# Gated recurrence, sparse and local attention in one transformer block: the recurrence's scores in column strips of 32 tokens, with its decays multiplied in place

## What is computed

```
f = lb + (1 - lb) * sigmoid(fp);  k = (1 - lb) * sigmoid(-fp)
b = cumsum(log f)
decay = exp(where(causal, b_i - b_j, -1e30))         # per channel d
scores_ij = sum_d q_id * decay_ijd * k_jd
o_i = sum_j scores_ij * v_j + (q_i * exp(b_i)) @ state
```

```
score = sum over 8 index heads of iw_h * relu(iq_h . ik)      # 64 channels per index head
keep the 64 largest scores of each row, softmax over those, times the compressed values
```

## Time and profile before

| | |
|---|---|
| median of 3 runs | 493.51 us |
| the profiled execution's own time | 493.7 us |
| its span | 491.9 us |
| TensorE busy (matmul) | 476.9 us, 97% of the span |
| TensorE weight loads | 398.2 us, 81% |
| VectorE busy | 306.7 us, 62% |
| ScalarE busy | 236.5 us, 48% |
| GpSimd busy | 64.8 us, 13% |
| mean granted TensorE clock | 0.991 |

### The profile page before, as it was taken

One profiled execution on the slowest core, in us unless ns is written; L12 is line 12 of the kernel. 1 busy time (PEld: TensorE's weight loads), 2 busy tenths in 40 slices (PEclk: granted clock), 3 DMA queues, 4 the chain that ended last, 5 costly groups with the idle time before them and its releaser, 6 DMA issues.

```text
span 491.9 us, 5942 instructions
## 1 busy us (share of the span) xinstructions
PE 476.9 (97%) x2292; PEld 398.2 (81%) x2292; DVE 306.7 (62%) x405; ACT 236.5 (48%) x330; POOL 64.8 (13%) x54
## 2 busy tenths in 40 slices
PE   7999999996999999999999999999999999999995
PEld 6888778885888888888888886888888888888884
DVE  5657679978447765467537787584644645643432
ACT  4948367162436555544455155565354453533520
POOL 0421001995470020000000000000000000000000
PEclk9999999997999999999999999999999999999999
DMA  8987635341233535566865634755565656565302
GB/s 299 401 254 215 190 128 172 113 139 50 85 111 107 182 117 171 172 193 216 282 205 178 204 102 164 228 199 176 182 200 173 197 185 183 190 228 179 122 0 85
DMA packets 25728, 85.71 MB, mean 174 GB/s; under 512 B 3011, under 2 KB 4580, under 8 KB 25700
## 3 DMA queue, kind: packets, MB, share of 16 engines
q1 hardware_dynamic: 24888, 84.39, 52.9%
q10 hardware_dynamic: 812, 0.95, 0.5%
HBM read 84.08 MB, written 1.25 MB: 173 GB/s over the span
## 4 chain that ended last, share of the span: by engine, by line
PE 84%; DVE 10%; ACT 2%; issue 1%; DMA 1%; DVEq 0%; ACTq 0%
PE bank L1262 75%; PE bank L1286 4%; DVE wl L700 3%; PE bank L1435 1%; DVE work L834 1%; DVE top L832 1%; PE bank L1376 1%; DMA cols<-cols_in 1%; ACT wh L428 1%; DVE prob L892 1%; PE bank L1407 1%; DVE prob L878 1%; PE bank L1349 1%; PE bank L1358 1%; ACT prob L532 1%
## 5 line engine op out<-in xcount | busy, mean ns | idle before, releaser
L700 DVE TENSOR_TENSOR wl<-raw,wh 128x1024 fp32r<-128x1024 f32 (+2 forms) x152 | 184.6, 1247 | 79.3 <-ACT wh L428 78.7
L428 ACT ACTIVATE wh<-raw 128x1024 fp32r<-128x1024 f32 (+2 forms) x152 | 153.7, 1046 | 62.1 <-PE bank L1262 62.0
L1262 PE MATMUL bank<-wh,hTh 128*128 128x512 f32 (+1 forms) x432 | 171.7, 398 | 2.0 <-DVE hTl L720 0.9
L1262 PE MATMUL bank<-wl,hTh 128*128 128x512 f32 (+1 forms) x432 | 167.8, 388 | 0.0
L1262 PE MATMUL bank<-wh,hTl 128*128 128x512 f32 (+1 forms) x432 | 167.7, 388 | 0.0
L1262 PEld LDWEIGHTS bank<-wh,hTh 128*128 128x128 f32 x432 | 81.6, 189 | 20.0 <-issue 1.3
L1262 PEld LDWEIGHTS bank<-wh,hTl 128*128 128x128 f32 x432 | 81.5, 189 | 16.8
L1262 PEld LDWEIGHTS bank<-wl,hTh 128*128 128x128 f32 x432 | 81.7, 189 | 15.2
L1198 POOL TENSOR_TENSOR st<-st 128x1 f32<-128x1 f32 x4 | 2.2, 549 | 290.9 <-DVE st L1107 170.9
L1262 PE MATMUL bank<-wh,fTh 128*128 128x512 f32 x88 | 34.7, 395 | 0.0
L1262 PE MATMUL bank<-wh,fTl 128*128 128x512 f32 x88 | 34.5, 392 | 0.0
(11 more groups left out here) (186 smaller groups left out, 486.3 us busy)
## 6 DMA issues: line engine op xcount, KB each, us to landing
raw<-w_stream SPq DMA_DIRECT2D x148, 512.0 KB, 3.6
raw<-w_stream SPq DMA_DIRECT2D x4, 328.0 KB, 8.6
x<-x_in SPq DMA_DIRECT2D x4, 256.0 KB, 5.6
bias<-bias_scratch SPq DMA_DIRECT2D x8, 128.0 KB, 5.1
x<-x_in SPq DMA_DIRECT2D x1, 1024.0 KB, 5.8
out<-mo SPq DMA_DIRECT2D x4, 256.0 KB, 2.0
post<-post_mix ACTq DMA_DIRECT2D x1, 512.0 KB, 8.7
fg<-pre_ffn SPq DMA_DIRECT2D x1, 512.0 KB, 6.6
```

The costliest lines, as they stand in the source:

```text
L428: did(act.activation(wh[:, u % SPLIT, a:2 * w], raw[:, u % RING, a:2 * w], ACT.Copy), high_done, u + 1)
L700: did(dve.tensor_tensor(wl[:, u % RING, a:2 * w], raw[:, u % RING, a:2 * w], wh[:, u % SPLIT, a:2 * w].bitcast(F32), ALU.subtract), low_do ...
L1262: ins = pe.matmul(bank[bk][:, 0:w], lhs[:, kt, t * P:(t + 1) * P], rhs[:, k], start=first, stop=final)
```

## The change

Five things change, all in front of the first gate block; the units, their order and all that follows are the same.

1. **Strips.** `diag` and the levels 1 to 16 are computed in strips of 32 tokens: for each head and token tile, four matmuls with 32 stationary columns (the strip's k) and 32 or 16 moving ones (the strip's q), which write partitions 32j to 32j + 31 of PSUM. Level 32 takes 16 matmuls of 32 by 32, level 64 takes 8 of 64 by 64, level 128 is as before. The scores of the levels up to 16 go into a compact tile `near` (128 x 8 x 32), which ScalarE spreads into `tri` at the end (`spread_near`); `tri` is cleared by GpSimd early on.
2. **In place.** GpSimd keeps `kT` and `qp` (q times gates) and multiplies the lower halves of one and the upper halves of the other by one gate product per half; the products of the halves (`f_up`) are one small multiplication per level. So a level can be built only when TensorE has finished the one before.
3. **Two units apart.** The levels now stand two units apart on TensorE, and the "d" attention's probabilities, values, and the "m" attention's logits move behind levels 32, 64 and 128; `mP` moves behind `ho`.
4. **Scaling and normalising on ScalarE.** The gates' scaling (8 operations) and the division by the sums (8 operations for each attention) move from VectorE to ScalarE; VectorE keeps the reciprocal (`invert_sums`).
5. **Indexer by row halves.** The matmuls of an even and an odd index head alternate, into two banks.

```diff
@@ tensor: indexer
-            for i in range(6):
-                if i % 2 == 0:
-                    units(15 + i // 2)
-                ps = begin(f"ix{i}")
-                t, its_heads = INDEXER[i]
-                w = 512 // len(its_heads)
-                for k, h in enumerate(its_heads):
+            for i in range(0, 6, 2):
+                units(15 + i // 2)
+                pair = [begin(f"ix{i}"), begin(f"ix{i + 1}")]
+                t, n = INDEXER[i][0], len(INDEXER[i][1])
+                w = 512 // n
+                for k in range(n):
+                    for ps, (_, its_heads) in zip(pair, INDEXER[i:i + 2]):
+                        h = its_heads[k]
...
@@ tensor: diag and level
+            tokens_of = [(h * TT + t, h, t) for h in range(H) for t in range(TT)]
+            ps = begin("diag")
+            for c, h, t in tokens_of:
+                for j in range(0, P, STRIP):
+                    at = slice(t * P + j, t * P + j + STRIP)
+                    ins = pe.matmul(ps[j:j + STRIP, c * STRIP:(c + 1) * STRIP], kT[:, h, at], hqT[:, h, at], start=True, stop=True)
...
-                for t in range(TT):
-                    for h in range(H):
-                        a_h = att[i % 2][:, h, t * P:(t + 1) * P]
-                        upper = a_h.rearrange("p (g two k) -> p g two k", two=2, k=w)[:, :, 1, :]
-                        at = t * S + h * P // 2
-                        ins = pe.matmul(ps[:, at:at + P // 2], a_h, upper, start=True, stop=True)
+                for c, h, t in tokens_of:
+                    if w in IN_STRIP:
+                        for j in range(0, P, STRIP):
+                            at = slice(t * P + j, t * P + j + STRIP)
+                            upper = qp[:, h, at].rearrange("p (g two k) -> p g two k", two=2, k=w)[:, :, 1, :]
+                            ins = pe.matmul(ps[j:j + STRIP, c * HALF_STRIP:(c + 1) * HALF_STRIP], kT[:, h, at], upper, start=True, stop=True)
+                    else:
+                        for j in range(0, P, 2 * w):
+                            a = t * P + j
+                            ins = pe.matmul(ps[j:j + w, c * w:(c + 1) * w], kT[:, h, a:a + w], qp[:, h, a + w:a + 2 * w], start=True, stop=True)
@@ gpsimd
-            for i, w in enumerate(LEVELS + [P]):
...
-                did(pool.tensor_tensor(a_lo, k_lo, s_lo, ALU.mult))
-                did(pool.tensor_tensor(a_up, q_up, p_up, ALU.mult), s["level_built"], i + 1)
...
-                    did(pool.tensor_tensor(s_lo, s_lo, p_up[:, :, w - 1:w].to_broadcast([P, g, w]), ALU.mult))
...
-                    did(pool.tensor_tensor(p_up, p_up, p_lo[:, :, w - 1:w].to_broadcast([P, g, w]), ALU.mult))
+            did(pool.memset(tri[:], 0.0), tri_zeroed, 1)
...
+            did(pool.tensor_tensor(qp[:], hqT[:], pre[:], ALU.mult), s["level_built"], 1)
+            for i, w in enumerate(LEVELS):
...
+                f_lo, f_up = (f[:, :, w - 1:w] for f in halves(pre[:], w))
+                wait_job(pool, f"L{w}")
...
+                did(pool.tensor_tensor(k_lo, k_lo, f_up.to_broadcast([P, g, w]), ALU.mult))
+                did(pool.tensor_tensor(q_up, q_up, f_lo.to_broadcast([P, g, w]), ALU.mult), s["level_built"], i + 2)
...
+                    did(pool.tensor_tensor(f_up, f_up, f_lo, ALU.mult))
@@ scalar
+            for h in range(H):
+                did(act.activation(kT[:, h], kT[:, h], ACT.Copy, scale=stat(OML + h)))
+                did(act.activation(pre[:, h], pre[:, h], ACT.Identity, bias=stat(LB + h), scale=stat(OML + h)), gates_scaled, h + 1)
...
+            def normalise(k):
+
+                act.wait_ge(sums_inverted, k + 1)
...
+                        ins = act.activation(row, row, ACT.Copy, scale=stat(RCP + 8 * k + t * H + h))
...
+                    did(act.activation(tri4[sl, :, 0:3:2, sl], near[sl].rearrange("p (h t) k -> p h t k", t=TT), ACT.Copy), tri_near, n + 1)
@@ vector: level
+                if w in IN_STRIP:
...
+                    did(dve.copy_predicated(upper, mask, src), *job_read(f"L{w}"))
+                    return
...
+                    ins = dve.tensor_copy(tri4[j:j + w, :, 0:3:2, j + w:j + 2 * w], src)
```

More of the change, by code:

```diff
@@ L200, in build_block @@
         pre = sb("pre", [P, H, S], stack=early)
-        suf = sb("suf", [P, H, S], stack=early)
-        att = [sb(f"att{i}", [P, H, S], stack=early) for i in range(2)]
+        qp = sb("qp", [P, H, S], stack=early)
+        near = sb("near", [P, H * TT, STRIP], stack=early)
         tri = sb("tri", [P, H, TW], stack=early)
@@ L939, in _ @@
             low_until(44)
-            normalise(1)
+            logits("m", 1, 0)
+            maxima(1)
             low_until(45)
@@ L1459, in _ @@
                 transposes(f"mqT{i}", tiles(stage[:, 2], 2 * i))
-            units(33)
+            units(34)
             level(4)
-            units(34)
-            level(5)
             units(35)
@@ L1468, in _ @@
             units(36)
+            level(5)
+            units(37)
+            pe.wait_ge(s["prob_ready"], 1)
+            prob_transposes("d")
+            units(38)
+            level(6)
+            units(39)
+            after_job(pe, "dP2")
+            after_job(pe, "vc1")
+            values("d", vc)
+            units(40)
+            pe.wait_ge(s["level_built"], len(LEVELS) + 1)
+            ps = begin("L128")
+            for h in range(H):
+                ins = pe.matmul(ps[:, h * P:(h + 1) * P], kT[:, h, 0:P], qp[:, h, P:S], start=True, stop=True)
+            end("L128", ins)
+            units(41)
             after_job(pe, "mqT1")
@@ L1471, in _ @@
             logits("m")
-            units(37)
-            level(6)
-            units(39)
-            pe.wait_ge(s["level_built"], len(LEVELS) + 1)
-            ps = begin("L128")
-            for h in range(H):
-                a_h = att[len(LEVELS) % 2][:, h, :]
-                ins = pe.matmul(ps[:, h * P:(h + 1) * P], a_h[:, 0:P], a_h[:, P:S], start=True, stop=True)
-            end("L128", ins)
-            units(42)
-            pe.wait_ge(s["prob_ready"], 2)
-            prob_transposes("m")
             units(43)
             after_job(pe, "L128")
+            pe.wait_ge(tri_near, NSTRIP)
             after_block(pe, "hi")
@@ L1497, in _ @@
                 end(f"ho{t}", ins)
-            units(44)
+            units(47)
+            pe.wait_ge(s["prob_ready"], 2)
+            prob_transposes("m")
+            units(49)
             after_job(pe, "mP2")
```

218 lines of the change are left out of this document (106 added, 112 removed), and 4 rows, old and new, of the table JOBS.

## The result

| | before | change |
|---|---|---|
| median | 493.56 us (4 runs, 492.88 to 493.84) | **476.95 us** (4 runs, 476.66 to 477.07) |
| ratio, 95% interval | | **0.9664** [0.9651, 0.9676] |
| span of the profiled execution | 491.9 us | 475.1 us |

The change makes the kernel 3.4% faster. I had forecast 486.5 us with a range from 479 to 499: the right direction, but less than half of the gain, and the result lies outside the range.

What follows compares the result with a forecast made beforehand. The prediction took TensorE to bound the kernel (97% busy). Removed waits -9.0, indexer -2.1 and strips +3.9 summed to -7.2 us, from 493.7 to 486.5 us, with a range from 479 to 499 us.

Steps and rivals of the forecast that it cites:

- p = 0.035 us: TensorE, strip visits: assumed time between two records, taken nearest to the row of 8-column loads.
- The strips: TensorE, diag and levels 1 to 64: 432 records plus eight shape changes replace 13.6 us; cost +3.9 us.
- strips load side by side: TensorE strip visits: neighbouring strips load in parallel, 0.015 to 0.02 us per record; total 477.9 to 480.1 us; chance 0.12.
- 432 p: TensorE, diag and levels 1 to 64: 432 records times the time between two records, forecast 15.1 us.
- first rival: TensorE strip visits: issuing, not loading, sets the pace, 0.05 us or more per record; 494.1 to 498.7 us; chance 0.28.
- The removed waits: TensorE, "d" transposes and unit 30: waits of 5.0 and 1.0 us plus 3.0 us of slow clock go; -9.0 us.
- The indexer: TensorE, three indexer visits: alternating even and odd heads lets row halves work side by side; -2.1 us.
- What costs nothing: GpSimd, VectorE and ScalarE work fits behind TensorE's units; unit 31's low part holds narrowly, 7.6 against 7.9 us.
- third rival: TensorE at unit 31's low part: new wait up to 1 us, clock fall another 3; 488 to 491 us; chance 0.08.
- The fourth: TensorE strip visits: columns do not matter, 0.106 us per record; +34.6 us, total 517.2 us; chance 0.05.
- What I said would show it: Trace signs: strip starts 0.035 us apart, large indexer visits 1.1 us, no "d" transpose wait, clock 1.0; over 10 us means cheap strips.
- second rival: TensorE strip visits: strips load in parallel as row halves do, cost -4.7 to -2.6 us; chance 0.12.

Runs made afterwards that it cites:

- the long execution above: Profiled execution of the change with VectorE's low parts of units 31 and 32 ahead of mask and maxima; that kernel's median 476.46 us, highest 477.75.

## Why the prediction was right and wrong

**The step that failed: p = 0.035 us, in the part "The strips".** I took it "nearest to the row of 8 columns", which gives 0.028 us for a load of 32 columns, plus a few ns. The price for one column group was sized right: with one group after the other a record takes 0.027 us, whatever its moving columns. That this is the load of the 32 stationary columns is likely but not shown; no run changes their number alone. What was wrong is how many go at once. I had named the possibility as a rival, "strips load side by side", and given it 0.12 with one sentence against it: "strips share all rows, the halves do not". That is no argument, as the run shows: strips that share all 128 rows but write other columns work four at a time, 0.009 us per record. In the sum, 432 p is 384 x 0.0088 + 32 x 0.017 + 16 x 0.061 = 4.9 instead of 15.1 us. Even the rival's lower end, 0.015, was too high, since it thought of two at once, as the row halves do, and not of four; at 0.015 the total stood at 477.9, and the range, from 479 us on, left out "half of the fast strips". (Two totals of the first rival, 494.1 and 498.7, start from 493.5 us, the others from 493.7; the 0.2 us change nothing.)

The Trainium skill had the rule for it, and I had weighed only the one against. TensorEngine Tiling (Array Packing), section "Tiling Modes", lists 128 rows by 32 columns as four tiles and says that "Different tiles can execute LdWeights and Matmul in parallel". The trace agrees: 0.009 us with four groups in turn, 0.027 with one. The Trainium skill's rule that I had quoted against the change, no matmul start within about 25 ns of the last (TensorE: Matmul & The Clock Gate, section "Wait — 56ns, not 53.3ns?"), fits at most one column group: 0.027 us on average there, 0.009 across groups. Of its 62 ns nothing is to be seen.

**The rest of that term.** The 0.30 us for changing the array's shape, read off one indexer visit in the earlier trace rows, was right: `diag` and level 1 in one visit save 0.29, and 0.87 less 64 x 0.0088 leaves 0.31. The eight old visits cost 14.3 us by the account's measure instead of the 13.6 that I counted to the next product only. So the term is 4.9 + 2.4 - 14.3 = -7.0 us, as measured, and not +3.9: of the 10.9 us between them 10.2 are p. They are the whole error and more; the new wait of 1.4 us took some of it back.

**The removed waits: right.** Forecast -9.0 (5.0 + 3.0 for the clock + 1.0), measured -7.9 - 1.0 = -8.9. The clock's part is confirmed by the kernel before with only the divisions moved, where wait and slow clock go together. The reason I gave was more than was needed: "the probabilities are wanted only after unit 37 instead of 30, and VectorE has less to do ahead of it". The first half is enough; with the division back on VectorE, done no earlier than before, the time is the same.

**The indexer: right.** -2.1 forecast, -2.3 in the account, 2.4 when put back. The visits end at 1.06 us, forecast 1.1.

**What costs nothing: right but for one.** GpSimd had its two units: its two operations for a level take 3.1 to 4.5 us, and no level waits for them. TensorE waits for nothing of ScalarE's or GpSimd's, so the room there and the clearing of `tri` hold as forecast. The exception is the place that I called late next, unit 31's low part. VectorE is ready 7.7 us after level 2's end (99.80 to 107.5; I had said 7.6). TensorE, which I had arriving after 7.9 us, arrives after 6.35 (99.80 to 106.15), as its level takes 0.67 and not 2.5 us: 1.3 us of waiting. So the wait of the third rival came true as well, "above all if the strips are fast", though not its 488 to 491 us, nor the fall of the clock that I had added to it. The windows of the trace show 1.00 across the wait:

```profile
104.50:110.00 5.50, 4.18 (x80) 3.23 (x79) 5.36 (x5) 4.91 (x19) 4.20 (x3) 1.00 0.55 177
```

A wait of 5.0 us in the earlier trace rows was followed by the lower clock, one of 1.3 here was not. The length of the wait alone does not decide: the two of 2.2 and 2.3 us in the kernel before with the strips alone were not either (1.00 from 102 to 113 us), while the one of 1.9 us in the first norm, in the long execution above, was followed by 0.50.

**The slower side.** The first rival (records that cost 0.05 us and more) had 0.28; nothing of it was seen. The fourth, columns do not matter, is refuted by the same rows.

**What I said would show it** did: "If the time falls by over 10 us, the strips were as cheap as the second rival says".

**Gains that do not add up one by one.** By spans: strips alone 3.4, divisions alone 6.8, indexer 2.2, sum 12.4 us; together 16.8. Of the missing 4.4 the visits ahead of the division are 3.7, which count only once nobody waits for VectorE there; the waits in front of unit 30 and for the second attention's division, which the change does not have, are 1.8, and its new one takes 1.4 back: 4.1. This is bookkeeping with measured terms; no run puts just two of the edits together.

## What to carry to other kernels

Split a small matmul whose wanted results lie in blocks on the diagonal into strips that write different groups of 32 PSUM partitions, and issue them in turn over the four groups: four records then cost about what one does (0.009 against 0.027 us each, for 32 stationary columns of float32), and half-height operands likewise by alternating the halves. Each visit in another shape cost 0.3 us here, so strips of several jobs belong in one visit. When TensorE gets faster, look again at what it used to arrive behind: the gain turned into waiting twice here (4.5 us in the kernel before with strips alone, where 0.8 had been, and 1.3 us in the change), and in the change moving two low parts ahead of the mask removed the wait.

## What the hardware showed unexpectedly

**Moving columns are nearly free in strips.** `diag` (32 moving columns) takes 0.90 us, a level (16) 0.87. Even with one column group after the other the two differ by 0.01 us.

**GpSimd's small operations do not get smaller.** The third operation of a level halves its size from level to level. Its time hardly moves (groups of GpSimd by shape, 80 to 140 us: busy us, mean ns, idle us before):

```profile
L1213 POOL TENSOR_TENSOR qp<-qp,pre 128x512 f32<-128x512 f32 x7 | 14.1, 2014 | 0.0
...
L1216 POOL TENSOR_TENSOR pre<-pre 128x512 f32<-128x512 f32 x1 | 1.2, 1238 | 0.1
L1216 POOL TENSOR_TENSOR pre<-pre 128x32 f32<-128x32 f32 x1 | 1.2, 1167 | 0.1
L1216 POOL TENSOR_TENSOR pre<-pre 128x16 f32<-128x16 f32 x1 | 1.1, 1111 | 0.1
```

16 elements take 1.11 us, 512 take 1.24. It is off the path here. Why the small ones, which read and write with a stride, are no faster was not tried.

**The same work on VectorE takes longer at one time than at another.** The two mask operations took 4.33 us from 100.17 in the change, and 2.25 us from 104.94 with the low parts ahead of them, which in turn took 4.87 us from 100.15, while a single one took 1.22 a little earlier, when GpSimd stood still. In both kernels GpSimd is at work from 99.96 to about 105 us; these are the first of the change's rows:

```profile
97.11 1.22 DVE L738 TENSOR_TENSOR wl<-raw,wh 128x1024 fp32r<-128x1024 f32 x1
...
99.96 1.52 POOL L1212 TENSOR_TENSOR kT<-kT,pre 128x512 f32<-128x512 f32 x1 [3.69 <-PE bank L1465]
101.44 1.98 POOL L1213 TENSOR_TENSOR qp<-qp,pre 128x512 f32<-128x512 f32 x1
```

That points to GpSimd holding VectorE up; no run here takes GpSimd away to show it. And it is not as simple as at work or not: GpSimd was busy in about 1.5 of the 2.25 us of the faster mask too. The Trainium skill, GPSIMD Engine Reference, section "Specifications", says that the two share their access to SBUF and get in each other's way where VectorE reads two inputs from there, as the mask and the low parts do; the low parts' rows agree (4.87 us for two beside GpSimd, 1.22 for one without it), the mask's do so only in part.
